# One 256-column PSUM accumulator for three products in a split-precision decoder trunk

## What is computed

```
h = x
for i in range(DEPTH):                       # DEPTH = 2
    hn = rms_norm(h, norm_mix_g[i])
    mix = conv_recurrent_mixer(...) if i % 2 == 0 else stick_breaking_mixer(...)
    h = h + mix
    h = h + squared_relu_mlp(rms_norm(h, norm_mlp_g[i]), w_mlp_up[i], w_mlp_down[i])   # 2048 -> 8192 -> 2048
    gate = jax.nn.sigmoid(rms_norm(h, norm_ple_g[i]) @ w_ple_gate[i])
    h = h + (p[i] @ w_ple_proj[i]) * gate
return rms_norm(h, norm_f_g)
```

## Time and profile before

| | us |
|---|---|
| median of 3 runs | 2427.11 |
| lowest and highest run | 2415.29, 2431.84 |
| profiled execution, first to last instruction | 2426.7 |
| TensorE busy in it | 2377.3 (98%) |
| VectorE, ScalarE busy in it | 1601.0 (66%), 1276.6 (53%) |
| mean granted TensorE clock | 0.994 of 2.4 GHz |

### The profile page before, as it was taken

How to read it: one execution, slowest core, us unless ns; L and a number is a source line. 1 busy time by engine, 2 the same in 40 slices (tenths; PEclk the granted TensorE clock), 3 DMA queues, 4 the chain that set the end, 5 groups by cost and what they waited for, 6 DMA issues and landing times.

```text
span 2426.7 us, 39317 instructions
## 1 busy us (share of the span) xinstructions
PE 2377.3 (98%) x13454; PEld 2064.3 (85%) x13454; DVE 1601.0 (66%) x1892; ACT 1276.6 (53%) x1632; POOL 2.1 (0%) x15
## 2 busy tenths in 40 slices
PE   7999999999999999999999999999999999999997
PEld 6878888888888888888888888888888888888886
DVE  8789986655555555667776766765556556556665
ACT  6665565444444444555565665555445444445553
POOL 0000000000000000000000000000000000000000
PEclk9999999999999999999999999999999999999998
DMA  7644456556565556555655554656565565565543
GB/s 233 204 130 137 133 163 193 188 183 188 183 188 184 185 186 186 182 189 169 194 180 168 167 156 146 197 180 194 185 186 188 185 185 187 184 187 182 188 159 104
DMA packets 432146, 431.03 MB, mean 178 GB/s; under 512 B 13136, under 2 KB 430032, under 8 KB 432080
## 3 DMA queue, kind: packets, MB, share of 16 engines
q1 hardware_dynamic: 432080, 430.20, 56.8%
HBM read 428.05 MB, written 2.10 MB: 177 GB/s over the span
## 4 chain that ended last, share of the span: by engine, by line
PE 92%; DVE 4%; ACT 2%; DMA 1%; issue 1%; DVEq 0%; SPq 0%; ACTq 0%
PE ps L399 56%; PE ps L400 28%; PE ps L396 2%; PE O L572 2%; PE ps L397 1%; DVE spl L1033 1%; ACT spl L632 0%; DMA raw<-in_w_o 0%; PE O L501 0%; DVE tv L1069 0%; PE Z L475 0%; DMA raw<-in_w_in 0%; PE ps L457 0%; DVE nacc L1097 0%; DVE h L1113 0%
## 5 line engine op out<-in xcount | busy, mean ns | idle before, releaser
L1033 DVE TENSOR_TENSOR spl<-raw,spl 128x1024 fp32r<-128x1024 f32 x810 | 980.1, 1223 | 543.3 <-ACT spl L632 517.5
L632 ACT ACTIVATE spl<-raw 128x1024 fp32r<-128x1024 f32 x810 | 842.4, 1054 | 708.8 <-PE ps L400 664.3
L399 PE MATMUL ps<-XA,spl 128*128 128x512 f32 x3072 | 1090.0, 400 | 15.4 <-DVE spl L1033 10.8
L399 PE MATMUL ps<-XB,spl 128*128 128x512 f32 x3072 | 1088.5, 399 | 0.5 <-DVE pp L1069 0.5
L400 PE MATMUL ps<-XA,spl 128*128 128x256 f32 x3072 | 863.4, 281 | 0.0
L400 PE MATMUL ps<-XB,spl 128*128 128x256 f32 x3072 | 862.4, 281 | 0.0
L399 PEld LDWEIGHTS ps<-XA,spl 128*128 128x128 f32 x3072 | 578.4, 188 | 158.8 <-issue 12.3
L399 PEld LDWEIGHTS ps<-XB,spl 128*128 128x128 f32 x3072 | 577.2, 188 | 143.5 <-issue 1.3
L400 PEld LDWEIGHTS ps<-XA,spl 128*128 128x128 f32 x3072 | 581.8, 189 | 0.4
L400 PEld LDWEIGHTS ps<-XB,spl 128*128 128x128 f32 x3072 | 580.4, 189 | 0.2
L1069 DVE TENSOR_TENSOR tv<-cross,ps 128x512 f32<-128x512 f32 x208 | 141.5, 680 | 41.0 <-ACT cross L632 40.8
(11 more groups left out here) (145 smaller groups left out, 892.6 us busy)
## 6 DMA issues: line engine op xcount, KB each, us to landing
raw<-in_w_up SPq DMA_DIRECT2D x256, 512.0 KB, 3.9
raw<-in_w_down SPq DMA_DIRECT2D x256, 512.0 KB, 3.5
raw<-in_w_qkv SPq DMA_DIRECT2D x96, 512.0 KB, 4.5
raw<-in_w_in SPq DMA_DIRECT2D x64, 512.0 KB, 4.4
raw<-in_w_gate SPq DMA_DIRECT2D x64, 512.0 KB, 4.2
raw<-in_w_out SPq DMA_DIRECT2D x32, 512.0 KB, 3.4
raw<-in_w_o SPq DMA_DIRECT2D x32, 512.0 KB, 4.6
raw<-in_w_proj SPq DMA_DIRECT2D x8, 512.0 KB, 4.3
```

The source lines that it names most:

```text
L399: pe.matmul(ps[:, b + o, :], w[:, q, 0, c], x[:, kt, :, :], start=start, stop=False)
L632: return act.activation(out, in_, ACT.Copy, scale=scale)
L1033: dve.tensor_tensor(s[:, :, 1, :], raw[:, m % NRAW, :, :], s[:, :, 0, :].bitcast(F32), ALU.subtract).then_inc(lo_ready, 1)
```

## The change

The three products go into one accumulator of 256 columns, by three matmuls of 256 columns each (`three`); the high weights are named as the stationary operand twice. A group's two halves of 128 output channels share one bank. `ps` then holds four groups, and group g waits for `acc_taken` of group g - 4. `take_cross`, `take_sum`, `cross` and `sum_ready` go; the first operation of each group reads PSUM itself. In `ple` ScalarE copies the sum to `pp` alone. `fold` becomes one addition of 512 columns into an `nacc` of twice the size, and `stats` two accumulating matmuls instead of one. `up` computes the high part as a square with rounding straight from `tv`. In `gate` and `out_groups` all four splits come ahead of the evacuation. Several loops are written out or get a body twice as long.

```diff
-        ps = ctx.enter_context(nc.psum_tensor("ps", [P, 4, 512], F32))
+        ps = ctx.enter_context(nc.psum_tensor("ps", [P, NACC, 2, 256], F32))     # NACC = 4
+            def three(out, a, b, start, stop):
+                pe.matmul(out, a[0], b[0], start=start, stop=False, skip_group_check=True)
+                pe.matmul(out, a[0], b[1], start=False, stop=False, skip_group_check=True)
+                return pe.matmul(out, a[1], b[0], start=False, stop=stop, skip_group_check=True)
 ...
-                            pe.matmul(ps[:, b + o, :], w[:, q, 0, c], x[:, kt, :, :], start=start, stop=False)
-                            mm = pe.matmul(ps[:, b + o, 0:256], w[:, q, 1, c], x[:, kt, 0, :], start=False, stop=stop)
+                        a, b = [w[:, q, k, c] for k in range(2)], [x[:, kt, k, :] for k in range(2)]
+                        mm = three(ps[:, g % NACC, o, :], a, b, first and q == 0 and o == 0, last and q == 3)
 ...
-                if counts(g - 1, gi):
-                    pe.wait_ge(sum_ready, gi + (g - 1))
+                if counts(gi + (g - 3)):
+                    pe.wait_ge(acc_taken, gi + (g - 3))
 ...
-                mm = pe.matmul(Z[:, 0, 0:256], onesD[:, :], nacc[:, :], start=True, stop=True)
+                for j in range(2):
+                    mm = pe.matmul(Z[:, 0, 0:256], onesD[:, :], nacc[:, j, :], start=(j == 0), stop=(j == 1),
+                                   skip_group_check=True)
 ...
-            def take_cross(g, gi, ready):
-                if counts(g, gi):
-                    act.wait_ge(sum_ready, gi + g)
-                act.wait_ge(*ready)
-                b = 2 * (g % 2)
-                copy(cross[:, :, :], ps[:, b:b + 2, 256:512]).then_inc(cross_copied, 1)
 ...
-                act.activation(tv[:, :, :], tv[:, :, :], ACT.Square).then_inc(up_sq, 1)
-                act.wait_ge(up_sq, u + 1)
-                copy(hid[:, bass.ds(t0, 2), 0, :], tv[:, :, :]).then_inc(up_hi, 1)
+                act.activation(hid[:, bass.ds(t0, 2), 0, :], tv[:, :, :], ACT.Square).then_inc(up_sq, 1)
+                act.activation(tv[:, :, :], tv[:, :, :], ACT.Square).then_inc(up_hi, 1)
 ...
-                dve.wait_ge(cross_copied, gi + (g + 1))
-                dve.tensor_tensor(tv[:, :, :] if out is None else out, cross[:, :, :], ps[:, b:b + 2, 0:256],
-                                  ALU.add).then_inc(sum_ready, 1)
 ...
-                dve.tensor_tensor(tv[:, 0, :], tv[:, 0, :], tv[:, 1, :], ALU.add).then_inc(sq_folded, 1)
-                dve.wait_ge(sq_folded, f * 2 + 1)
-                dve.tensor_tensor(nacc[:, :], nacc[:, :], tv[:, 0, :], ALU.add).then_inc(sq_folded, 1)
+                dve.tensor_tensor(nacc[:, :, :], nacc[:, :, :], tv[:, :, :], ALU.add).then_inc(sq_folded, 1)
 ...
             def gate(...):                                                   # on VectorE
-                group(g, gi, m, it, first, 2)
+                group(s, m, it, first)                                       # all four splits, then the wait for the group
...
-                scaled(g, gi, tv[:, :, :], gate_scaled)
-                if not first:
-                    split(m + 2 + NSPL, it)
+                scaled(g, tv[:, :, :])
 ...
+                    act.wait_ge(*((ple_done, 7 * layer + u + 1) if u < 7 else (chunk_used, m + 5)))
+                    copy(pp[:, 2 * u:2 * u + 2, :], ps[:, (g + u) % NACC, :, :]).then_inc(acc_taken, 1)
```

More of the change, by code:

```diff
@@ L506, in mlp @@
             def mlp(g, m, x, hid, f_in, norm, u):
[L507 to L513, removed]
+                after_norm(g, m, x, f_in, norm)
+                with pe.Fori(0, 2) as i:
+                    for s in range(4):
+                        gemm(g + 8 + s, i * 4, m + 32 + 4 * s, i * 2, hid,
                              [(up_tiles, u + 2 * j + 2) for j in range(4)])
                 with pe.Fori(1, 4) as f:
[L516 to L521, removed]
+                    with pe.Fori(0, 2) as i:
+                        for s in range(4):
+                            gemm(g + s, f * 16 + i * 4, m + 4 * s, f * 8 + i * 2, x)
+                    with pe.Fori(0, 2) as i:
+                        for s in range(4):
+                            gemm(g + 8 + s, f * 16 + i * 4, m + 32 + 4 * s, f * 8 + i * 2, hid,
                                  [(up_tiles, f * 8 + (u + 2 * j + 2)) for j in range(4)])
@@ L578, in _ @@
             gemm(G_GLU + 1, 0, C_GLU + 4, 0, XA)
-            with pe.Fori(1, 4) as c:
+            for c in range(1, 4):
                 for s in range(2):
@@ L617, in _ @@
             pair(1, 0, False)
-            with pe.Fori(1, 4) as i:
+            for i in range(1, 4):
                 pair(0, i, False)
@@ L818, in rec_pair @@
                 m = C_REC + NSPL + 8 * c
-                for q in range(4):
-                    split(m + q)
-                take_cross(G_REC + 2 * c, 0, group_done(C_REC + 8 * c, 0))
-                for q in range(4, 6):
+                for q in range(6):
                     split(m + q)
@@ L982, in qkv @@
                 if first and part < 2:
-                    group(g, 0, m, 0, True)
+                    group(part, m, 0, True)
                 else:
@@ L989, in qkv @@
                             steps[q](s - 1, i)
-                        split(m + NSPL + q, i * 3)
-                if not (first and part < 2):
-                    take_cross(g, i * 6, group_done(m, i * 3))
+                        split(m + NSPL + q)
                 if first and part == 0:
                     norm(3, columns=True)
-                act.wait_ge(qk_scaled, i * 6 + (3 * s + part + 1))
+                taken(g, 0)
                 out = vv[s][:, :, 0, :] if part == 2 else qk[s][:, part, :, 0, :]
@@ L1001, in _ @@
                     qkv(part, s, 0, first=(s == 0))
-            with act.Fori(1, 4) as i:
+            for i in range(1, 4):
                 for s in range(2):
@@ L1147, in gate, with out_groups @@
                 dve.wait_ge(gate_mul, k + 1)
-                add_h(hidx, t0)
-                if not first:
-                    split(m + 3 + NSPL, it)
+                add_gated(g, k, t0)
                 residual(f, t0, n, X)
-            def out_groups(g, m, hidx, f, n, X, first=None):
+            def out_groups(g, m, f, n, X, first=None):
                 clear(n)
@@ L1157, in out_groups @@
                     for s in range(2):
-                        down(g + s, 0, m + 4 * s, 0, hidx + s, 2 * s, True, steps=first)
+                        down(g + s, 0, s, m + 4 * s, 0, 2 * s, True, steps=first)
                         residual(f + s, 2 * s, n, X)
-                with dve.Fori(1 if first else 0, 4) as i:
-                    for s in range(2):
-                        down(g + s, i * 2, m + 4 * s, i, i * 2 + (hidx + s), i * 4 + 2 * s, later=1)
-                        split(m + 4 * s + 3 + NSPL, i)
-                        residual(i * 2 + (f + s), i * 4 + 2 * s, n, X)
@@ L1190, in gates @@
[L1190 to L1198 removed]
+                for s in range(2 if first else 0, 8):
+                    down(g + s, 0, s % 2, m + 4 * s, 0, 2 * s)
+                    residual(f + s, 2 * s, n, X)
@@ L1202, in _, with gates @@
+            def gates(g, m, k, f, norm_in, n, X):
+                for s in range(8):
+                    gate(g + s, 0, s % 2, m + 4 * s, 0, k + s, f + s, 2 * s, n, X,
+                         norm_in if s == 0 else None, s < 2)
             lam = params[:, LAMBDA:LAMBDA + 8]
@@ L1530, in _ @@
                     qkv(part, s, 0, first=(s == 0))
-            with dve.Fori(1, 4) as i:
+            for i in range(1, 4):
                 for s in range(2):
```

438 lines of the change are left out of this document (194 added, 244 removed).

## The result

The changed kernel takes 2469.35 us (median of 4 runs, 2468.8 to 2471.6), against 2421.2 us of before in the same comparison: ratio 1.0228, 95% interval 1.0168 to 1.0289 (an estimate from the single runs; the quotient of the two medians is 1.0199). It is slower, as forecast, and by more than forecast (2460/2427.11 = 1.0136); whether by more than 2%, the interval leaves open. Its profiled execution took 2469.69 us with a span of 2467.9, 41.2 us more than the 2426.7 of the profile before. The width of the interval is the kernel before's: its runs lie between 2399 and 2432, those of the changed kernel within 3 us. Why is the second finding of this study.

A forecast was written before the change was run, and what follows sets the result against it. TensorE's matmul stream was taken as the bound: 46.5 + 2.6 - 2.9 - 7 - 0.8 - 1.3 - 0.9 = +36.2 us on 2426.7 gave 2463, lowered to 2460 us for a pace slightly under 120; range 2410 to 2475.

The forecast's parts named there:

- the twelve matmuls of the earlier trace: Last twelve of 18 successive 256-column matmuls (L552), 120.0 ns each; taken as the pace of the new triples.
- the term of +46.5 us: TensorE's large products: 6464 triples at 360 ns instead of pairs at 352.8; low end -11.6 us.
- Rivals A and C: TensorE's stream: A, pace stays, 2415 or 2405 us, chance 0.17; C, 118 to 119.3 ns average, 2434 us, 0.18.
- Parts 2 to 4: Extra statistics matmul +2.6 us, fewer PSUM waits -2.9 and -7, shorter chains -0.8, -1.3 and -0.9.
- embedding, both layers: Per-layer embedding: four banks and one ScalarE copy let groups run ahead; -7 us, between 0 and -12.
- convolution and the wait ahead of it: Wait for the convolution's matrices: ScalarE has up to two copies less ahead of it; -1.3 us.
- start to the first statistics matmul: First norm, paced by split and fold in turn: 0.15 us saved for each of six, -0.9 us.
- last statistics matmul but one to the end: Kernel's end: copy, sum and hand-overs go, fold shortens, second statistics matmul adds some 0.85 us; -0.8 us.
- waits on a sum -2.9: Two TensorE waits on the sum that frees a bank, 1.42 and 1.45 us, lose their cause; together -2.9 us.
- statistics +2.6: Norms: a second 256-column statistics matmul adds about 0.43 us on the full clock, six norms in the stream; +2.6 us.
- The order at a group's end: gate and out_groups: splits ahead of evacuation cost 0, covered by PSUM room; without cover 2 us at six stage ends.
- Rival B: TensorE's longer loop bodies: instruction fetches at ten to twenty jumps back add 15 to 60 us, 2475 to 2520; chance 0.09.

The follow-up runs named there:

- e1: The kernel before with only chunk's 512-column matmul cut into two of 256 columns, the embedding's 64 pairs unchanged: 2473.2 us, ratio 1.0234.
- e3: The changed kernel with TensorE's outer loop over the three later quarters of each MLP written out, inner loops kept: 2455.5 us.
- e8: The changed kernel with TensorE's outer MLP loop written out, and PSUM room for two groups instead of four (NACC = 2): 2482.52 us.
- e10: The kernel before, unchanged, profiled again: 2414.13 us, first MLP in the slow rhythm and second in the fast.

## Why the prediction came out as it did

**The bound and the pace: right.** TensorE's stream decided, and the twelve matmuls of the earlier trace rows gave its new pace to the nanosecond. "At 120 a triple costs 360 ns" holds; the term of +46.5 us measured 45.3 (e1). Rivals A and C are refuted: no stage settled at 117 or 118. What they had for them, that a 256-column matmul can take anything from 0.11 to 0.12 us, was true only among 512-column ones. The fixed cost of 2.5 ns per matmul of the Trainium skill (TensorE: Matmul & The Clock Gate, "Back-to-back issue gap") would, as an estimate from that page, have made it 16 us; the same section calls its formula the gap of an isolated matmul, and says that it counts too little at small N where each matmul has its load. e1 says 45, so the measurement decides against the formula for this stream.

**The idle time: right in sign, under-sized.** Parts 2 to 4 came to -10.3 us. Against the same pace, e3 less e1, they measured 2453.4 - 2472.0 = -18.6. The starts of the stages in both traces say where:

| stretch | forecast | e3 less e1 |
|---|---|---|
| embedding, both layers | -7 | -11.5 |
| convolution and the wait ahead of it | -1.3 | -2.6 |
| start to the first statistics matmul | -0.9 | -1.6 |
| last statistics matmul but one to the end | -0.8 | -0.5 |
| all else (waits on a sum -2.9, statistics +2.6) | -0.3 | -2.4 |

The mis-sized term is the embedding's: its waits fell from 9.0 to 2.1 us, and the lower clock behind them went too, of which I had priced only a part. The wait ahead of the convolution fell by 1.1 us, near the forecast, but it now ends with the gated input from VectorE. The extra statistics matmul shows in the two MLPs, where neither kernel waits: each is 0.3 to 0.4 us longer, 0.43 forecast.

**The order at a group's end: right with its condition.** "Cost 0" rested on the cover by 34 us of room. Without the room it costs more than my six times 2 us: e8 is 29.1 us slower, 22 of them outside the embedding. I had left out that the second pair waits too, and the clock.

**Rival B was not a rival but a term: the first step that failed.** I gave it 0.09 as an alternative outcome and put it at nothing in the sum. It happened beside the forecast, at two jumps instead of ten to twenty, for +14.5 us (e3). I had named the place (the jump back over a longer body), priced a jump at 1.4 to 3.9 us where each took 7, and left it out of the sum, because one short burst without a hole spoke against it; a burst of 18 without a jump in it could not.

The three measured parts are 45.3 - 18.6 + 14.5 = 41.2 us, the difference of the spans. They are steps from before to e1 to e3 to the changed kernel, so they must add up; that they do confirms nothing. My sum had 46.5 - 10.3 = 36.2, went down to 33 for a pace of 119.8 that no stage showed, and had no third part. Two misses partly cancel, 8 us more saved than forecast and 14.5 of holes that the sum left out: that 2469.35 us is only 9 over the forecast is in part luck.

**The base: the second step that failed.** "The profiled span is within 0.4 us of the median, so nothing is added." In microseconds 2469.35 lies in the range of 2410 to 2475. As a ratio it does not: 1.0228 is beyond 2475/2427.11 = 1.0197, though the lower end of its interval, 1.0168, is not. It took both steps: 2469.35 against the base of 2427.11 would be 1.0174, and e3, without the holes, against this comparison's 2421.2 would be 1.0142, both inside. The median of three runs was one from the slowest of three groups, and so was the profile; the median of the later 13 was 2415.3. The range of the three, 2415 to 2432, held two groups already, and the profile held both rhythms. I averaged them into 352.8 ns instead of asking what the time would be if the rhythm fell the other way: 13.6 us for each MLP. Against that median of 2415.3 the change costs 54 us: 41 by the profiles, 13 because before is usually in a faster rhythm than its profile was.

**What stays open.** Why a stream of 256-column fp32r matmuls settles at 120 ns, 8 above the floor of 112, and what chooses between 347 and 353 for long and short ones in turn, no run here shows. That the holes are fetches of instructions fits the jump, the "issue" label and the length of the body; shown is only that they go with the jump. That the pieces on the instruction queue rose says little, as they rose again in e3, which has no holes. Why the granted clock fell with 128 columns while nothing waited is open too.

## What to carry to other kernels

When a stream of matmuls bounds a kernel, price a new form by the longest stretch of that same form in the trace, start to start, and look for runs long enough to settle. Cutting one 512-column matmul into two costs even though no column is added (here 7 to 13 ns for each), and no saving on VectorE or ScalarE pays for it when they were waiting anyway. Before forecasting one or two per cent, ask whether the runs of before stand in groups, and whether a rhythm in the profile explains them; a mere change of order (two long, two short) can fix the rhythm, here 0.5% under the median, though not under the fastest runs. After writing out or lengthening loops on the engine that is the bound, count the instructions of the longest body that is jumped back over (here 768 matmuls and loads never waited, 1536 did at two of four jumps).

## What was not expected of the hardware

- One instruction stream has two stable rhythms: 346.7 and 353.3 ns for a pair of 512 and 256 columns, kept over 2033 pairs. In the three profiles of before it never changes inside an MLP, but where other matmuls come between: at the norm's float32 matmul (at 1110 us in all three, at 1612 us in e10) and between groups of the attention. The runs' three groups, 14 us apart, fit it; two of them have a profile. Two long and two short in turn gave one rhythm (348 ns) and ten runs within 2.7 us.
- In a row of matmuls with a weight load each, 1, 128 and 240 columns all take 112 ns; 248 take 115 and 256 take 120.
- With 128 columns the granted clock was 0.50 from 1200 to 1300 us, in a stream without an idle stretch.
- A jump back over a body of some 1540 instructions stopped TensorE at both jumps of the first MLP, for 7 us each with the lower clock, and never in the second, which has a copy of the same loop at another place of the instruction list.
